# The heads of two feed-forwards without GpSimd, and the squaring of their hidden tiles on ScalarE

## The chip, the cores and the metric

The kernel runs on one core of a Trainium2 chip. The metric is the device time of one launch in microseconds. The kernel before takes 4710.16 us, the median of three runs of 4697.45, 4710.16 and 4712.71 us.

## The reference

Three blocks follow one another over a sequence of 1024 tokens of width 1024: a mixer with three groups of recurrences, a block with a short convolution and an attention, and a block with two gated mixers. The second and the third block each hold a feed-forward with a hidden width of 4096, and the change touches these two alone:

```
m = rmsnorm(h, g_mlp[i])
h = h + jnp.square(jax.nn.relu(m @ w_up[i])) @ w_down[i]
```

```
def rmsnorm(x, g):
    y = xf * lax.rsqrt(jnp.mean(xf * xf, axis=-1, keepdims=True) + EPS)
    return (y * g.astype(jnp.float32)).astype(x.dtype)
```

A token's root factor is the same for all its hidden values, so it can be put on behind the up product: with s = 1/sqrt(mean + eps), relu(u s)^2 is relu(u)^2 s^2, and it is also (relu(u) s)^2.

## The kernel before

Both feed-forwards are built by one function, `feed_forward`, called as "2" and as "3". The residual stream `all_hid` stands in SBUF with channels on the partitions: 8 tiles of 128x1024. All large products are done in three passes, as high*high, low*high and high*low: each operand is rounded to a high part by ScalarE, and VectorE makes the low part as the value less the high part. So nothing can be multiplied before ScalarE and then VectorE have passed over it.

The up product makes the hidden tiles in pairs, 16 pairs of two tiles (128x1024 each). Pairs 0 and 1 are made plainly (`multiply_plain`, line 3068): four blocks u of the weights, 24 matmuls each. From pair 2 on (PLAIN = 2) a pair is a 2x2 block product after Strassen in Winograd's form: seven products j = 0 to 6 (`multiply`, line 3095) of 12 matmuls of 128x512 each, where the right-hand sides are four sums and differences of blocks of x, and the left-hand sides are four sums and differences of blocks of the weights (`combine`). In the kernel before all the weight sums and nine of the ten instructions of the x sums are on GpSimd (POOL); the x sums read copies of the scaled x that ScalarE lays down first (`scale_x`, 12 instructions). The tenth (`t3`, line 3354) is on VectorE. TensorE takes the first products of pair 2 in the order j = 0, 1, 2, 3, ..., and each of j = 1 to 4 waits there for its x sum (`t_low`).

The results of the seven products lie in four PSUM banks (`ff_bank`). ScalarE reads the ones of j = 0, 1, 2 and 6 into `ff_made_out` (`read`, line 3174), VectorE adds those of 3, 4 and 5 (line 3317). TensorE's product 3 uses the bank of product 1 again and so waits for the read of product 1. Then `shape` makes the hidden tile: line 3327 takes max(a, 0) * a, line 3331 multiplies by the row `all_sums`, which holds 1/(mean + eps). SyncE stores the tile to DRAM (`inner`, line 3007).

Order is written out by hand: each engine works off one list of its own, and semaphores tie the lists together. Of the lists these points matter:

- SyncE: for each pair q it stores the first tile, loads the raw up-weights of pair q + 2 (two DMAs of 512 KB into the one buffer `ff_raw`, line 3003), and stores the second tile. The load waits until VectorE has made the low part of the sixth block of pair q + 1 (semaphore `w_low`). After the last pair's predecessor it goes on to `load_y` (line 3027) and `load_w` (line 3017) of the down product: tiles y0, y1, weights w0, y2 to y5, w1, y6 to y9, the store of tile 31, y10 to y13, the store of tile 30, w2.
- ScalarE: a pair's list is read 0, high 0, read 1, high 1, read 2, high 2 to 5, read 6, high 6. A high part of pair q + 1 waits for the same product of pair q, whose weights it replaces.
- The down product (line 3116) makes 32 output parts of 128x1024 in 48 matmuls each, eight parts for each quarter of the hidden tiles. The first part needs y0 to y7 one after another, with 6 matmuls for each.

The row itself is made once: the squares' sums are totalled by TensorE (line 225, 8 matmuls for both feed-forwards), and ScalarE takes Ln (line 233) and Exp (line 235).

Of the kernel before, what the change touches and what calls it, by code (L numbers as in the profile page):

```python
# [2939 lines left out]
def feed_forward(nc, dram, n, hid, gain, up, down, sums):  # L2940
# [8 lines left out]
    with Part(nc, "ff" + n, dram) as p:  # L2949
# [11 lines left out]
        (combined, w_high, w_low, x_high, x_low, scaled, summed_x, third, t_high, t_low, product, act_read, dve_read, shaped, made) = (  # L2961
            p.sem(a) for a in ("combined", "w_high", "w_low", "x_high", "x_low", "scaled", "summed_x", "third", "t_high", "t_low",
# [4 lines left out]
        scale = TokenScale(nc, p, sums, row, power=-1.0, total=acc[:, 0])  # L2967
# [86 lines left out]
        def _(pe):  # L3054
# [17 lines left out]
            def multiply(q, j):  # L3072
# [17 lines left out]
                if q == PLAIN and j in (1, 2, 3, 4):  # L3090
                    pe.wait_ge(t_low, {4: 1, 2: 2, 1: 3, 3: 4}[j])
# [31 lines left out]
        def _(act):  # L3123
            A = nc.scalar.activation
            nc.scalar.preload_act_table_set("natural_log_exp_and_others")

# [23 lines left out]
            def scale_x(h):  # L3150
                A(x_hi[:, 2:4, h, :], cut(hid[:, h, :]), ACT.Copy, scale=gain[:, h:h + 1]).then_inc(scaled, 1)
                lower, g = cut(hid[:, h + H, :]), gain[:, h + H:h + H + 1]
                A(x_hi[:, 4, h, :], lower[:, 1, :], ACT.Copy, scale=g).then_inc(scaled, 1)
                A(x[:, 3, h, :], lower[:, 0, :], ACT.Copy, scale=g).then_inc(scaled, 1)

            def high_t(t, j, what):
                if j == 1:
                    act.wait_ge(summed_x, 1)
                    act.wait_ge(product, products(1) + 3)
                else:  # L3160
                    act.wait_ge(third, 2 * H if j != 3 else 2 * H + 1)
                    act.wait_ge(summed_x, 1)
# [23 lines left out]
            for u in range(2):  # L3186
                high_plain(0, u)
                for h in range(H):
                    high_x(u * H + h)
            high_plain(0, 2)  # L3190
            high_plain(0, 3)
            scale.root(act)
            copy(0, 0)
            for h in range(H):
                scale_x(h)
            high_plain(1, 0)
            high_plain(1, 1)
            copy(0, 1)
            high_plain(1, 2)
            high_plain(1, 3)  # L3200
            copy(1, 0)
            high(PLAIN, 0)
            high_t(0, 4, x[:, 4])
            high_t(1, 2, x[:, 2])
            high(PLAIN, 1)
            high_t(2, 1, t3)
            high_t(3, 3, x[:, 3])
            high(PLAIN, 2)
            copy(1, 1)
# [12 lines left out]
            for i in range(2, 6):  # L3222
# [3 lines left out]
            high_y(6)  # L3226
            high_y(7)
# [21 lines left out]
        def _(pool):  # L3249
            T = nc.gpsimd.tensor_tensor  # L3250

            def combine(q):
                pool.wait_ge(raw_in[0], 16 * q)
                if q > PLAIN:
                    pool.wait_ge(product, products(q - 1) + 2)
                T(wl[:, 1], a11, a21, ALU.subtract).then_inc(combined, 1)
                pool.wait_ge(raw_in[1], 16 * q)
                pool.wait_ge(combined, sums_made(q) + 1)
                T(a21, a21, a22, ALU.add).then_inc(combined, 1)
                if q > PLAIN:  # L3260
                    pool.wait_ge(product, products(q - 1) + 3)
                pool.wait_ge(combined, sums_made(q) + 2)
                T(wl[:, 2], a21, a11, ALU.subtract).then_inc(combined, 1)
                if q > PLAIN:
                    pool.wait_ge(w_low, products(q))
                pool.wait_ge(combined, sums_made(q) + 3)
# [570 lines left out]
```

## Time and profile before

| | |
|---|---|
| median of three runs | 4710.16 us |
| the profiled execution | 4700.76 us, of which its span 4699.0 us |
| TensorE (PE) busy | 4270.1 us, 91% of the span |
| VectorE (DVE) busy | 2091.5 us, 45% |
| ScalarE (ACT) busy | 1603.2 us, 34% |
| GpSimd (POOL) busy | 636.8 us, 14% |
| mean granted TensorE clock | 0.958 of full speed |

The times of one execution are counted from the start of its span. Feed-forward 2 lies from about 2629 to 3315 us, feed-forward 3 from about 3981 us to near the end. Busy shares are means over many stages; for the change it counts where TensorE stands still inside these two stretches. A matmul's own duration in the trace (390 ns) is longer than the distance of two starts, since they overlap; the distance is what counts.

### The profile page before, as it was taken

Reading aid. Unit: us, or ns where it says so; the run is one execution under the profiler, and the core shown is the slowest. Engines: PE = TensorE matmul, PEld = TensorE weight load, DVE = VectorE, ACT = ScalarE, POOL = GpSimd, SP = SyncE. Lnnn points to the kernel's source line nnn. Section 1 sums busy time; section 2 is a strip of 40 time slices with the busy share of each in tenths; the row PEclk is TensorE's granted clock in tenths of the full one; section 3 lists DMA queues with packets and bytes.
Section 4 is the critical chain, followed back from the end, with each engine's and each line's share of the span. In section 5 each row is a group of like instructions: output and inputs, shape, how many; then the busy total and the mean of one; then the engine's idle time right before and its main releaser. Section 6 shows DMA issues by size and latency. Waiting matters only on the chain. (4 is left out here: it accounts for less than half of the span.)

```text
span 4699.0 us, 67316 instructions
## 1 busy us (share of the span) xinstructions
PE 4270.1 (91%) x28429; PEld 3475.5 (74%) x28429; DVE 2091.5 (45%) x2868; ACT 1603.2 (34%) x2680; POOL 636.8 (14%) x508
## 2 busy tenths in 40 slices
PE   7988899987979979899998899999989878999998
PEld 5988889756958858677434688888767676788887
DVE  4544425363345552324443466433442363666333
ACT  3732235242243332311575433222332333433221
POOL 0024400010001100002231332000100001321001
PEclk8989999998989999999999999999999898999999
DMA  3110012122110021111000133421111221234222
GB/s 112 38 60 2 2 41 70 49 65 81 45 36 9 9 78 45 62 42 45 32 10 27 56 115 108 148 95 59 53 33 41 57 47 45 94 112 153 82 94 72
DMA packets 323010, 284.91 MB, mean 61 GB/s; under 512 B 19569, under 2 KB 288145, under 8 KB 322594
## 3 DMA queue, kind: packets, MB, share of 16 engines
q1 hardware_dynamic: 322722, 280.76, 19.3%
q8 instruction: 218, 3.57, 0.3%
q14 instruction: 70, 0.57, 0.0%
HBM read 204.55 MB, written 55.31 MB: 55 GB/s over the span
## 5 line engine op out<-in xcount | busy, mean ns | idle before, releaser
L3116 PE MATMUL ff_acc<-ff_x_hi_rounded,ff_wh_rounded 128*128 128x512 f32 x1024 | 399.8, 390 | 5.2 <-DVE ff_x_rounded L3335 5.2
L3116 PE MATMUL ff_acc<-ff_x_rounded,ff_wh_rounded 128*128 128x512 f32 x1024 | 399.2, 390 | 0.0
L3116 PE MATMUL ff_acc<-ff_x_hi_rounded,ff_wl_rounded 128*128 128x512 f32 x1024 | 399.2, 390 | 0.0
L3095 PE MATMUL ff_bank<-ff_x_hi_rounded,ff_wh_rounded 128*128 128x512 f32 x784 | 308.8, 394 | 17.0 <-issue 9.6
L3095 PE MATMUL ff_bank<-ff_x_hi_rounded,ff_wl_rounded 128*128 128x512 f32 x784 | 308.0, 393 | 0.0
L3095 PE MATMUL ff_bank<-ff_x_rounded,ff_wh_rounded 128*128 128x512 f32 x784 | 308.0, 393 | 0.0
L3116 PEld LDWEIGHTS ff_acc<-ff_x_hi_rounded,ff_wh_rounded 128*128 128x128 f32 x1024 | 192.7, 188 | 46.8 <-DVE ff_x_rounded L3335 6.9
L3184 ACT ACTIVATE ff_wh_rounded<-ff_wl 128x512 fp32r<-128x512 f32 x128 | 80.6, 632 | 417.2 <-DMA ff_wl<-w_mlp_dram 207.7
L3116 PEld LDWEIGHTS ff_acc<-ff_x_hi_rounded,ff_wl_rounded 128*128 128x128 f32 x1024 | 192.7, 188 | 39.9
L3116 PEld LDWEIGHTS ff_acc<-ff_x_rounded,ff_wh_rounded 128*128 128x128 f32 x1024 | 192.6, 188 | 39.9
L3405 DVE TENSOR_TENSOR all_hid<-all_hid,ff_acc 128x1024 f32<-128x1024 f32 x64 | 78.2, 1221 | 303.0 <-PE ff_acc L3116 303.0
L1936 PE MATMUL mid_acc<-b1h_hn_hi_rounded,mid_w_hi_rounded 128*128 128x352 f32 (+1 forms) x528 | 186.8, 354 | 4.7 <-DVE mid_w_rounded L1918 4.7
L3095 PEld LDWEIGHTS ff_bank<-ff_x_hi_rounded,ff_wh_rounded 128*128 128x128 f32 x784 | 149.0, 190 | 49.3 <-issue 18.6
L1936 PE MATMUL mid_acc<-b1h_hn_hi_rounded,mid_w_rounded 128*128 128x352 f32 (+1 forms) x528 | 183.8, 348 | 0.0
L1936 PE MATMUL mid_acc<-b1h_hn_rounded,mid_w_hi_rounded 128*128 128x352 f32 (+1 forms) x528 | 183.4, 347 | 0.0
L3095 PEld LDWEIGHTS ff_bank<-ff_x_rounded,ff_wh_rounded 128*128 128x128 f32 x784 | 148.9, 190 | 31.5
L3095 PEld LDWEIGHTS ff_bank<-ff_x_hi_rounded,ff_wl_rounded 128*128 128x128 f32 x784 | 149.1, 190 | 31.1
L3342 DVE TENSOR_TENSOR ff_wl_rounded<-ff_wl,ff_wh_rounded 128x512 fp32r<-128x512 f32 x128 | 98.5, 778 | 141.5 <-ACT ff_wh_rounded L3184 138.8
L1936 PE MATMUL pa_acc<-b1h_hn_hi_rounded,pa_w_hi_rounded 128*128 128x352 f32 x432 | 147.3, 341 | 12.0 <-DVE b1h_hn_rounded L1922 12.0
L477 PE MATMUL pb_acc<-b1h_hn_hi_rounded,pb_w_hi_rounded 128*128 128x352 f32 x408 | 132.8, 325 | 16.1 <-ACT b1h_hn_hi_rounded L381 16.1
L1936 PE MATMUL pa_acc<-b1h_hn_hi_rounded,pa_w_rounded 128*128 128x352 f32 x432 | 140.0, 324 | 0.0
L1936 PE MATMUL pa_acc<-b1h_hn_rounded,pa_w_hi_rounded 128*128 128x352 f32 x432 | 139.8, 324 | 0.0
(642 smaller groups left out, 10628.6 us busy)
## 6 DMA issues: line engine op xcount, KB each, us to landing
inner<-ff_made_out SPq DMA_DIRECT2D x64, 512.0 KB, 2.6
ff_x<-inner SPq DMA_DIRECT2D x64, 512.0 KB, 5.6
ff_wl<-w_down_dram SPq DMA_DIRECT2D x64, 256.0 KB, 3.1
ff_wl<-w_mlp_dram SPq DMA_DIRECT2D x64, 256.0 KB, 3.0
ff_raw<-w_up_dram SPq DMA_DIRECT2D x30, 512.0 KB, 4.2
ff_raw<-w_mlp_dram SPq DMA_DIRECT2D x30, 512.0 KB, 4.3
mid_w<-w_in_dram SPq DMA_DIRECT2D x104, 128.0 KB, 2.7
pa_w<-w_in_dram SPq DMA_DIRECT2D x72, 128.0 KB, 2.7
```

The costliest lines, as they stand in the source:

```text
L477: mm = nc.tensor.matmul(acc[s][:, c, :width], rounded(l[:, k, :]), rounded(r[:, k, at]), start=(k == 0 and j == 0), stop=(k == k_tiles - 1 ...
L1936: mm = self.nc.tensor.matmul(self.acc[s][:, c, :width], rounded(l[:, k, :]), rounded(r[:, k, at]), start=(k == 0 and j == 0), stop=(k == K ...
L3095: mm = M(to, rounded(a[:, j, h, :]), rounded(b[:, j, h, :]), start=(j in (0, 1, 5) and h == 0 and i == 0), stop=(h == H - 1 and i == 2), s ...
L3116: mm = M(acc[:, s, c, :], rounded(a[:, s, k, :]), rounded(b[:, at, c * W2:(c + 1) * W2]), start=(k == 0 and i == 0), stop=(k == KD - 1 and ...
L3184: A(rounded(w_hi[:, s, a * H:(a + 1) * H, :]), w[:, s, a * H:(a + 1) * H, :], ACT.Copy).then_inc(d_high, 1)
L3342: T(rounded(w[:, s, part, :]), w[:, s, part, :], rounded(w_hi[:, s, part, :]), ALU.subtract).then_inc(d_low, 1)
L3405: T(cut(hid[:, f, :]), cut(hid[:, f, :]), acc[:, s, :, :], ALU.add).then_inc(acc_free, 1)
```

## The change

In both feed-forwards:

- GpSimd does nothing any more before the down product's sums of squares. The four weight sums of a pair go to VectorE, in two pieces behind the low parts 0 and 1 of the pair. The x sums go to VectorE as 16 instructions of 128x512 (`sum_x`), which scale and subtract in one; ScalarE's `scale_x` shrinks from 12 instructions to 4 and stands ahead of the row's Ln and Exp. The t_low order becomes 4, 2, 3, 1.
- ScalarE and VectorE take x tiles 0 and 1 and x tile 0 ahead of the first weight block.
- The loading of a table of ScalarE's functions at the head (line 3125) goes.
- Hidden tiles: the row holds 1/sqrt(mean + eps) (the default power). In pairs 0 and 1 ScalarE rectifies as it copies out of PSUM and VectorE multiplies by the row (`weigh_plain`); in the others one instruction of VectorE takes max(a, 0) * row. In all pairs ScalarE squares the tile in place (`square_made`), and the store waits for that. In the pairs' lists the square of a pair's first finished tile stands behind high 5 of the next pair's weights, that of its second tile behind high 1 of the round after; the last ones stand behind the reads of pair 15 and behind the high parts of y0 to y7, w0 and w1.
- At the start of the down product the high and low parts of y6 and y7 stand ahead of w1 and of the last tiles' shaping.

```
-        scale = TokenScale(nc, p, sums, row, power=-1.0, total=acc[:, 0])
+        scale = TokenScale(nc, p, sums, row, total=acc[:, 0])
...
-            nc.scalar.preload_act_table_set("natural_log_exp_and_others")
...
             def copy(q, i):
                 act.wait_ge(product, products(q) + 2 * (i + 1))
-                A(cut(made_out[:, q % 2, i, :]), plain_acc[q, i], ACT.Copy).then_inc(act_read, 1)
+                A(cut(made_out[:, q % 2, i, :]), plain_acc[q, i], ACT.Relu).then_inc(act_read, 1)
+
+            def square_made(q, i):
+                act.wait_ge(shaped, 2 * q + (1 if i == first_half(q) else 2))
+                A(made_out[:, q % 2, i, :], made_out[:, q % 2, i, :], ACT.Square).then_inc(made, 1)
...
                     high(q + 1, j)
+                    if j == 1:
+                        square_made(q - 1, 1 - first_half(q - 1))
+                    if j == 5:
+                        square_made(q, 1)
             for j in range(3):
                 read(LAST, j)
+            square_made(LAST - 1, 0)
             high_y(0)
...
+            def combine(q, j):
+                if j == 1:
+                    for a in range(2):
+                        dve.wait_ge(raw_in[a], 16 * q)
+                    if q > PLAIN:
+                        dve.wait_ge(product, products(q - 1) + 2)
+                    T(wl[:, 1], a11, a21, ALU.subtract).then_inc(combined, 1)
+                    dve.wait_ge(combined, sums_made(q) + 1)
+                    T(a21, a21, a22, ALU.add).then_inc(combined, 1)
+                else:
+                    if q > PLAIN:
+                        dve.wait_ge(product, products(q - 1) + 3)
+                        dve.wait_ge(w_low, products(q))
+                    dve.wait_ge(combined, sums_made(q) + 2)
+                    T(wl[:, 2], a21, a11, ALU.subtract).then_inc(combined, 1)
+                    dve.wait_ge(combined, sums_made(q) + 3)
+                    T(fourth[:, :, :], a12, wl[:, 2], ALU.subtract).then_inc(combined, 1)
...
+            def sum_x(to, k, c, less):
+                V.scalar_tensor_tensor(to, hid[:, k, c * W2:(c + 1) * W2], gain[:, k:k + 1], less, ALU.mult, ALU.subtract).then_inc(summed_x, 1)
...
-                a = made_out[:, q % 2, i, :]
-                V.scalar_tensor_tensor(a, a, 0.0, a, ALU.max, ALU.mult).then_inc(shaped, 1)
-                dve.wait_ge(shaped, 2 * q + (1 if i == first_half(q) else 2))
-                if q == 0:
-                    dve.wait_ge(scale.rooted, 1)
-                T(a, a, row, ALU.mult).then_inc(made, 1)
+                a = made_out[:, q % 2, i, :]
+                V.scalar_tensor_tensor(a, a, 0.0, row, ALU.max, ALU.mult).then_inc(shaped, 1)
```

SyncE's and TensorE's lists keep their instructions and their order. Two places of the other lists bear on the time.

VectorE at the head of feed-forward 2, before. `ff_wl_rounded` are low parts of the weights, `ff_x_rounded` of x or an x sum, `ff_square<-ff_x_hi` is the sum t3, and the pairs of rows on `ff_made_out` are the shaping in two steps:

```order
L3293 TENSOR_TENSOR ff_wl_rounded<-ff_raw,ff_wh_rounded 128x512
L3304 SCALAR_TENSOR_TENSOR ff_x_rounded<-all_hid,all_par,ff_x_hi_rounded 128x2x512 x4
L3293 TENSOR_TENSOR ff_wl_rounded<-ff_raw,ff_wh_rounded 128x512
L3304 SCALAR_TENSOR_TENSOR ff_x_rounded<-all_hid,all_par,ff_x_hi_rounded 128x2x512 x4
L3293 TENSOR_TENSOR ff_wl_rounded<-ff_raw,ff_wh_rounded 128x512 x2
L3327 SCALAR_TENSOR_TENSOR ff_made_out<-ff_made_out 128x1024
L3331 TENSOR_TENSOR ff_made_out<-ff_made_out,all_sums 128x1024
L3293 TENSOR_TENSOR ff_wl_rounded<-ff_raw,ff_wh_rounded 128x512 x2
L3354 TENSOR_TENSOR ff_square<-ff_x_hi 128x2048
L3327 SCALAR_TENSOR_TENSOR ff_made_out<-ff_made_out 128x1024
L3331 TENSOR_TENSOR ff_made_out<-ff_made_out,all_sums 128x1024
L3293 TENSOR_TENSOR ff_wl_rounded<-ff_raw,ff_wh_rounded 128x512 x2
```

And in the changed kernel, where the rows on `all_par` of 128x512 are `sum_x`:

```order
L3303 SCALAR_TENSOR_TENSOR ff_x_rounded<-all_hid,all_par,ff_x_hi_rounded 128x2x512
L3274 TENSOR_TENSOR ff_wl_rounded<-ff_raw,ff_wh_rounded 128x512
L3303 SCALAR_TENSOR_TENSOR ff_x_rounded<-all_hid,all_par,ff_x_hi_rounded 128x2x512 x3
L3274 TENSOR_TENSOR ff_wl_rounded<-ff_raw,ff_wh_rounded 128x512
L3303 SCALAR_TENSOR_TENSOR ff_x_rounded<-all_hid,all_par,ff_x_hi_rounded 128x2x512 x4
L3274 TENSOR_TENSOR ff_wl_rounded<-ff_raw,ff_wh_rounded 128x512 x2
L3307 SCALAR_TENSOR_TENSOR ff_x<-all_hid,all_par,ff_x_hi 128x512 x4
L3307 SCALAR_TENSOR_TENSOR ff_square<-all_hid,all_par,ff_x_hi 128x512 x4
L3323 TENSOR_TENSOR ff_made_out<-ff_made_out,all_sums 128x1024
L3307 SCALAR_TENSOR_TENSOR ff_x<-all_hid,all_par,ff_x 128x512 x4
L3274 TENSOR_TENSOR ff_wl_rounded<-ff_raw,ff_wh_rounded 128x512 x2
L3307 SCALAR_TENSOR_TENSOR ff_x<-all_hid,all_par,ff_x 128x512 x4
```

One x tile has gone ahead of the first weight block, sixteen `sum_x` stand around the first tile's weighing, and t3 as one large instruction is gone.

ScalarE around the last pair of feed-forward 2, before: reads of `ff_bank`, the high parts of the hidden tiles (`ff_x_hi_rounded<-ff_x 128x1024`) and of the down weights (`ff_wh_rounded<-ff_wl`, twice):

```order
L3174 ACTIVATE ff_made_out<-ff_bank 128x512 x3
L3178 ACTIVATE ff_x_hi_rounded<-ff_x 128x1024 x2
L3184 ACTIVATE ff_wh_rounded<-ff_wl 128x512 x2
L3178 ACTIVATE ff_x_hi_rounded<-ff_x 128x1024 x4
L3184 ACTIVATE ff_wh_rounded<-ff_wl 128x512 x2
L3174 ACTIVATE ff_made_out<-ff_bank 128x512
L3178 ACTIVATE ff_x_hi_rounded<-ff_x 128x1024 x3
```

And in the changed kernel, where `ff_made_out<-ff_made_out` is a square:

```order
L3170 ACTIVATE ff_made_out<-ff_bank 128x512 x3
L3163 ACTIVATE ff_made_out<-ff_made_out 128x1024
L3174 ACTIVATE ff_x_hi_rounded<-ff_x 128x1024 x2
L3180 ACTIVATE ff_wh_rounded<-ff_wl 128x512 x2
L3174 ACTIVATE ff_x_hi_rounded<-ff_x 128x1024 x6
L3180 ACTIVATE ff_wh_rounded<-ff_wl 128x512 x2
L3170 ACTIVATE ff_made_out<-ff_bank 128x512
L3163 ACTIVATE ff_made_out<-ff_made_out 128x1024 x2
```

A square now stands between the three reads and the first y tile, SyncE's store and all its later loads wait for it, and y6 and y7 are ahead of w1.

## Rows read from the trace of the kernel before

**Rows 1.** Waits of TensorE, head of feed-forward 2; us in total, times, longest.

```profile
...
PE ff_bank L3095 <- DVE ff_x_rounded L3311: 3.5, 1, 3.5
PE ff_acc L3068 <- DVE ff_x_rounded L3304: 2.2, 1, 2.2
PE ff_acc L3068 <- DVE ff_wl_rounded L3293: 1.2, 1, 1.2
PE ff_bank L3068 <- DVE ff_wl_rounded L3293: 1.1, 1, 1.1
```

**Rows 2.** Waits of TensorE, 2700 to 2965 us.

```profile
PE ff_bank L3095 <- issue: 4.6, 1, 4.6
```

**Rows 3.** Waits of TensorE, head of feed-forward 3.

```profile
...
PE ff_bank L3095 <- issue: 5.0, 1, 5.0
PE ff_bank L3095 <- DVE ff_x_rounded L3311: 3.9, 1, 3.9
...
```

**Rows 4.** Timeline of TensorE, feed-forward 2: start us, duration us, instruction [idle <-releaser].

```profile
...
2659.54 0.39 PE L3068 MATMUL ff_bank<-ff_x_rounded,ff_wh_rounded 128*128 128x512 f32 x1
...
2715.11 0.39 PE L3095 MATMUL ff_bank<-ff_x_hi_rounded,ff_wh_rounded 128*128 128x512 f32 x1
...
```

**Rows 5.** Timeline of TensorE, feed-forward 3, the same two places.

```profile
...
4011.14 0.39 PE L3068 MATMUL ff_bank<-ff_x_rounded,ff_wh_rounded 128*128 128x512 f32 x1
...
4068.84 0.39 PE L3095 MATMUL ff_bank<-ff_x_hi_rounded,ff_wh_rounded 128*128 128x512 f32 x1
...
```

**Rows 6.** Windows: length, PE, PEld, DVE, ACT, POOL busy; PEclk, DMA share, GB/s.

```profile
2690.00:2695.00 5.00, 4.23 (x13) 3.38 (x14) 4.97 (x5) 0.05 (x1) 0.00 (x0) 0.71 0.00 0
2955.00:2960.00 5.00, 5.00 (x24) 4.15 (x23) 2.97 (x4) 4.11 (x5) 0.00 (x0) 1.00 1.04 413
4325.00:4330.00 5.00, 2.40 (x6) 1.94 (x7) 4.79 (x5) 0.00 (x0) 0.00 (x0) 0.71 0.90 365
```

**Rows 7.** Timeline of ScalarE, head of feed-forward 2.

```profile
...
2629.13 1.28 ACT L3125 ACT_TABLE_LOAD   x1 [3.39 <-PEq L155]
2632.04 0.63 ACT L3133 ACTIVATE ff_wh_rounded<-ff_raw 128x512 fp32r<-128x512 f32 x1 [1.62 <-DMA ff_raw<-w_up_dram]
...
2701.47 0.63 ACT L3144 ACTIVATE ff_wh_rounded<-ff_raw 128x512 fp32r<-128x512 f32 x1 [11.43 <-DMA ff_raw<-w_up_dram]
2702.01 0.58 ACT L3174 ACTIVATE ff_made_out<-ff_bank 128x512 f32<-128x512 f32 x1
...
```

**Rows 8.** Timeline of VectorE, head of feed-forward 2.

```profile
...
2659.73 2.92 DVE L3293 TENSOR_TENSOR ff_wl_rounded<-ff_raw,ff_wh_rounded 128x512 fp32r<-128x512 f32 x2 [7.09 <-ACT ff_wh_rounded L3133]
...
2665.87 5.62 DVE L3327 SCALAR_TENSOR_TENSOR ff_made_out<-ff_made_out 128x1024 f32<-128x1024 f32 x1
...
2695.74 1.89 DVE L3299 TENSOR_TENSOR ff_wl_rounded<-ff_raw,ff_wh_rounded 128x512 fp32r<-128x512 f32 x3
...
```

**Rows 9.** Timeline of SyncE: the loads of the up-weights of pairs 3, 6, 7.

```profile
...
2697.65 0.93 SPq L3003 DMA_DIRECT2D ff_raw<-w_up_dram  x2
...
2752.98 0.94 SPq L3003 DMA_DIRECT2D ff_raw<-w_up_dram  x2
...
2772.02 0.93 SPq L3003 DMA_DIRECT2D ff_raw<-w_up_dram  x2
...
```

**Rows 10.** Groups of VectorE, 2710 to 2945 us: busy us, mean ns | idle.

```profile
...
L3299 DVE TENSOR_TENSOR ff_wl_rounded<-ff_raw,ff_wh_rounded 128x512 fp32r<-128x512 f32 x51 | 34.9, 684 | 0.0
L3327 DVE SCALAR_TENSOR_TENSOR ff_made_out<-ff_made_out 128x1024 f32<-128x1024 f32 x25 | 30.6, 1222 | 0.4
...
```

**Rows 11.** Page, costliest groups: the down product's first line.

```profile
...
L3116 PE MATMUL ff_acc<-ff_x_hi_rounded,ff_wh_rounded 128*128 128x512 f32 x1024 | 399.8, 390 | 5.2 <-DVE ff_x_rounded L3335 5.2
...
```

**Rows 12.** Timeline of SyncE, start of the down product.

```profile
...
2948.47 1.14 SPq L3027 DMA_DIRECT2D ff_x<-inner  x2
...
```

**Rows 13.** Timeline of ScalarE, start of the down product.

```profile
2953.57 1.06 ACT L3178 ACTIVATE ff_x_hi_rounded<-ff_x 128x1024 fp32r<-128x1024 f32 x1 [1.02 <-DMA ff_x<-inner]
```

**Rows 14.** Timeline of VectorE, start of the down product.

```profile
...
2972.60 3.49 DVE L3335 TENSOR_TENSOR ff_x_rounded<-ff_x,ff_x_hi_rounded 128x1024 fp32r<-128x1024 f32 x3
...
```

More of the change, by code:

```diff
@@ L2960, in feed_forward @@
         stored = [p.sem(f"stored{s}") for s in range(2)]
-        (combined, w_high, w_low, x_high, x_low, scaled, summed_x, third, t_high, t_low, product, act_read, dve_read, shaped, made) = (
-            p.sem(a) for a in ("combined", "w_high", "w_low", "x_high", "x_low", "scaled", "summed_x", "third", "t_high", "t_low",
+        (combined, w_high, w_low, x_high, x_low, scaled, summed_x, t_high, t_low, product, act_read, dve_read, shaped, made) = (
+            p.sem(a) for a in ("combined", "w_high", "w_low", "x_high", "x_low", "scaled", "summed_x", "t_high", "t_low",
                                "product", "act_read", "dve_read", "shaped", "made"))
@@ L3184, in high_w @@
                     A(rounded(w_hi[:, s, a * H:(a + 1) * H, :]), w[:, s, a * H:(a + 1) * H, :], ACT.Copy).then_inc(d_high, 1)
[L3186 to L3189, printed above, removed]
+            high_x(0)
+            high_x(1)
+            high_plain(0, 0)
+            for k in range(2, H):
+                high_x(k)
+            high_plain(0, 1)
+            for k in range(H, KD):
+                high_x(k)
             high_plain(0, 2)
             high_plain(0, 3)
+            for h in range(H):
+                scale_x(h)
             scale.root(act)
             copy(0, 0)
-            for h in range(H):
-                scale_x(h)
             high_plain(1, 0)
             high_plain(1, 1)
+            square_made(0, 0)
             copy(0, 1)
@@ L3200, in _ @@
             high_plain(1, 3)
-            copy(1, 0)
-            high(PLAIN, 0)
             high_t(0, 4, x[:, 4])
             high_t(1, 2, x[:, 2])
+            high_t(2, 3, x[:, 3])
+            square_made(0, 1)
+            high(PLAIN, 0)
+            copy(1, 0)
             high(PLAIN, 1)
-            high_t(2, 1, t3)
-            high_t(3, 3, x[:, 3])
             high(PLAIN, 2)
+            high_t(3, 1, t3)
+            square_made(1, 0)
             copy(1, 1)
@@ L3221, in _ @@
             high_w(0)
-            for i in range(2, 6):
+            for i in range(2, KD):
                 high_y(i)
@@ L3250, in _ @@
             T = nc.gpsimd.tensor_tensor
[L3252 to L3266, printed above, removed]
-                T(fourth[:, :, :], a12, wl[:, 2], ALU.subtract).then_inc(combined, 1)
-            for h in range(H):
-                pool.wait_ge(scaled, 3 * h + 2)
-                T(x[:, 4, h, :], x_hi[:, 3, h, :], x_hi[:, 2, h, :], ALU.subtract).then_inc(third, 1)
-                pool.wait_ge(third, 2 * h + 1)
-                T(x[:, 2, h, :], x_hi[:, 4, h, :], x[:, 4, h, :], ALU.subtract).then_inc(third, 1)
-            pool.wait_ge(scaled, 3 * H)
-            pool.wait_ge(third, 2 * H)
-            T(x[:, 3], x[:, 3], x[:, 2], ALU.subtract).then_inc(third, 1)
-            for q in range(PLAIN, PAIRS):
-                combine(q)
             for f in range(KD):
@@ L3371, in _ @@
                     low(q + 1, j)
+                    if j < 2:
+                        combine(q + 1, j + 1)
                 read(q, 3)
@@ L3388, in _ @@
             shape(LAST, 1)
-            for i in range(3, 6):
+            for i in range(3, KD):
                 low_y(i)
```

72 lines of the change are left out of this document (38 added, 34 removed).

## Prediction

> **What bounds the kernel now.** I read the page's table of busy shares first: TensorE is busy 91% of the span, the others half of it or less. So the next view is who TensorE waits for inside the two feed-forwards. In feed-forward 2 the reader is to see few rows: at the head 2.2 us until the first low x tile, 1.2 and 1.1 us for low parts of pair 1's weights, 3.5 us for the low part of an x sum [rows 1], then 4.6 us of "issue" [rows 2], and after that nothing until the down product. Pairs 3 to 14 stand exactly 19.04 us apart (2772.02 less 2752.98) [rows 9]; that is 84 matmuls at 0.2267 us, TensorE at its own pace. Feed-forward 3 shows the same waits, 3.9 and 5.0 us for the two large ones [rows 3]. Each has one more at the start of the down product, 5.2 us for both together [rows 11].
>
> The timeline of TensorE gives the whole loss of the head in one subtraction. From the last matmul of pair 0 (2659.54) to the first of pair 3 (2715.11) there are 181 steps (the 96 matmuls of pair 1 and the 84 of pair 2 lie between); at 0.2267 us they take 41.0 us, and the rows are 55.6 us apart. So 14.5 us are lost: 10.4 in the four waits named, the rest in slow stretches behind the waits [rows 1, 2, 4]. The granted clock says the same, 0.71 of full over the window from 2690, where the engine had just stood still 3.5 us; a mean of its two levels, 2.4 and 1.2 GHz [rows 6]. In feed-forward 3 the same two places are 57.7 us apart, a loss of 16.7 us [rows 5].
>
> "Issue" names nobody, so the other engines' timelines have to. ScalarE takes a high part of pair 3's weights at 2701.47 after 11.4 us of idling for the DMA of `ff_raw`, and reads PSUM at 2702.01 [rows 7]; that read is the one that frees the bank of product 1, which product 3 writes. TensorE goes on at its end, 2702.6. The DMA was issued at 2697.65 [rows 9], because VectorE made low parts 3, 4 and 5 of pair 2 only from 2695.74 on [rows 8]. So both large waits have one cause: VectorE comes late. It comes late because it shares with GpSimd: one instruction of 128x1024 at 2665.87 took 5.62 us [rows 8], the same form takes 1.22 us in the steady pairs [rows 10].
>
> **The change part by part.** *The first product.* ScalarE idles 1.62 us for the first weights, behind a table load of 1.28 us [rows 7]. Now it makes the high parts of x0 and x1 there (1.06 us each, the row of the same form [rows 13]), and VectorE the low part of x0. The first product then hangs on the weights: 2632.04 + 0.63 + 0.69 = 2633.4 instead of 2635.2. These 1.7 us are at half clock. If the clock rises at the same instant as before, they are worth half, if it follows the start, all. I take 1.0 us (bounds 0.8 and 1.8).
>
> The table load itself costs nothing where it stands, since the DMA ended later. The trace has 1.28 us of load and then the DMA's wait. The Trainium skill ("ScalarE: Activation LUTs", What ACT_TABLE_LOAD costs) counts a drain of 1.38 us with each load, 2.66 us in all. By that rule on the path, the head would gain up to 2.7 us a time instead of 1.0, 3.4 us more for both; here the DMA row overrules it.
>
> *VectorE at the head.* It gets 16 `sum_x`. No row shows this form at 128x512; the nearest are 0.68 us for two tensors of 128x512 [rows 10] and 1.22 us as upper end (twice the elements). That is 10.9 us at the nearest, 19.5 us at most; I take the nearest. They fall where VectorE idled 7.1 us until 2659.73 and 4.9 us before its first shaping, and it loses t3, the waits beside GpSimd (5.62 - 1.22 = 4.4 us on one instruction alone) and three instructions of shaping. Counting its list through from 2633, at 1.22 us for 1024 elements and 0.64 for 512: the low x tiles end at 2642.5, the first eight `sum_x` at 2648.8, the weighing and four more at 2653, low parts 0 and 1 of pair 1 at 2654.1. Pair 1 is wanted at 2658.7 (2659.8 less the 1.0). There are 4.6 us to spare, so the 1.1 us wait goes; even at 1.22 us each it is late by about 1.3 us. Low parts 2 and 3 follow the third product's end at 2661.8, wanted at 2669.6. The three x sums' low parts (2.2 us each alone) end by 2671, the weight sums (four of 0.69) by 2674, low 1 and 2 at 2675.3, the fourth x sum at 2679.5; wanted for product 1 at 2683.2. So the 1.2 and the 3.5 us go, with the slow stretch behind.
>
> *What is late next.* Low 3 to 5 of pair 2 stand behind the weighing of pair 1's last tile, which needs pair 1's last product. From that product's end: ScalarE's copy 1.1, weighing 1.2, three low parts 1.9 [rows 8], the DMA 3.8 (2701.47 less 2697.65), the high part 0.6, the read 0.6, in all 9.3 us. TensorE has three products meanwhile, 3 x 2.72 = 8.2 us. A wait of 1.3 us stays in front of product 3 instead of 4.6. Then one more: ScalarE's next high part needs a weight sum, which VectorE makes only when both halves are in; with the second half a good 1 us behind the first, I get 0.7 us before product 4. In feed-forward 3 the load took some 0.4 us more, so 2.6 us there. Waits of 1.1 to 1.2 us left no slow stretch before, so I count none. Bounds for these waits: 0, and 5 us a head if transfers land 2 us later and the clock falls.
>
> Head: 14.5 + 1.0 - 2.0 = 13.5 us, and 16.7 + 1.0 - 2.6 = 15.1 us.
>
> *Steady pairs.* VectorE: two steps of shaping a tile become one (-2.4 us a pair), four weight sums come (+2.7). ScalarE: two squares, +2.1 us of 19. Neither is near 19 us, so only chains count, and I cost this at nothing. The cover: ScalarE's read of product 2 now stands behind a weight sum of VectorE, a high part and a square, 0.7 + 0.6 + 1.1 = 2.4 us after product 1; product 2 lasts 2.72 and product 3 another 2.72, before which nobody wants that read. What is queued behind the new waits on VectorE (for both halves of `ff_raw`) are low 1 and the reads of products 3 to 5, wanted a product or more later. The load of the next weights is issued behind a store that now waits for a square: product 5's end + 0.6 + 1.1 + 0.4 = 2.1 us. The bound above nothing is the first rival.
>
> The same page of the Trainium skill (Rules for kernel authors) says to put maximum and multiplication on VectorE rather than ScalarE, as VectorE is up to 3 times as fast in bf16. In fp32 the rows don't bear it out: 1.06 us on ScalarE [rows 13] against 1.22 on VectorE [rows 10] for 1024 elements. By the rule the two squares of a pair would slow ScalarE, but with 8 of 19 us busy the sum is the same.
>
> *Start of the down product.* Pair 15 starts at 2715.11 + 12 x 19.04 = 2943.6; its products end at 2946.4, ..., 2951.9 (third), 2962.8. SyncE loaded y0 at 2948.47 [rows 12]; now tile 28's store ahead of it waits for a square behind the third read: 2951.9 + 0.6 + 1.1 + 0.4 = 2954.0, so 5.5 us later. y0 landed 5.1 us after its issue (2953.57) [rows 13], now 2959.1. The queue then moves 413 GB/s at a DMA share of 1.04 [rows 6], 1.27 us for 512 KB. The weights w0 are third: 2961.6, high and low part to 2963.2; the product starts 0.4 us late. y7 is tenth: 2959.1 + 9 x 1.27 = 2970.5, ready at 2973.0; TensorE, with 1.36 us a tile, wants it at 2972.7. With small waits on the way the first part ends at about 2974.9. Before it ended at 2976.6: VectorE shaped the last tile ahead of y6, whose low part began at 2972.60 and ended at 2973.8 [rows 14], and two tiles of 1.36 us follow. That is 1.7 us gained. In feed-forward 3 the wait also cost a slow stretch (clock 0.71 from 4325 [rows 6]): six or seven matmuls at twice the distance, 1.3 us. Against it: w2 is queued behind the last two stores and y10 to y13, 3.4 MB from 2974.7 on, and lands about 2985, a moment after it could be used without loss (wanted, split, at 2985.8). I take 0.7 us for it, bounds 0 and 3. Net 1.0 and 2.3 us.
>
> **Sum.** 13.5 + 15.1 + 1.0 + 2.3 = 31.9 us. Against the profiled execution (4700.76) that is 4668.9 us; this execution was 9.4 us under the median of the runs, so against the median of 4710.16 it is 4678 us.
>
> **The rivals.** *A, slower: the store in front of the raw load.* Each pair the load shares the DMA engines with a store issued 0.4 us ahead (1.8 us before), and ScalarE's and VectorE's lists are blocked while they wait for it. From product 5's end, ScalarE must have done the next high 0 and read 1 when product 2 of the next pair ends, 4 x 2.72 = 10.9 us. Less 2.1 until the issue and 1.2 for the two instructions, the load may take 7.6 us; the row shows 3.8. Each us beyond 7.6 costs 1 us in 26 pairs. It decides from about 8.8 us, where the gain is eaten; at 9.5 us the kernel takes 4678 + 50 = 4728 us. Against it: two loads and a store are 1.5 MB, 3.8 us at 413 GB/s. *B, the down product starves.* The loads are 5.5 us later and TensorE waits for all of it, as the queue is already full before: 5.5 + 1.7 us each, with slow stretches 8.5; 32 - 17 gives 15 less, 4693 us. For it: the DMA share of 1.04. Against it: the wait before was for VectorE, not for a landing. *C, the heads stay bound by VectorE.* `sum_x` at 1.22 us and slow landings: 1.3 + 5 us a head come back, and the clock falls behind one of the waits (1.5): 32 - 16 = 16, 4694 us; with B in part it reaches no change. *D, the change doesn't do what it says:* without GpSimd at work the VectorE instructions stay long. Then it wasn't sharing, and the head would gain only the waits at pair 1, 4700 us. The same form at 1.22 us in steady pairs speaks against it.
>
> **How the numbers follow.** Forecast 0.70, A 0.05, B 0.12, C 0.09, D 0.04. The range must reach B and C, 4694, with some us for how the runs scatter (the three differ by 15 us), and down to 4661: start worth 1.8, no waits left, w2 in time, and the runs at the low end. So 4661 to 4700 us. A gain of 0.3% (14 us, what this kernel's measurement can tell) ends at 4696: the forecast, most of B and half of C are faster, 0.84; within 0.3% 0.10; slower 0.06.
>
> **What would show it.** TensorE's waits of 3.5 and 4.6 us gone, one of 1 to 2 us before product 3 of pair 2, and pair 3 starting 72 to 73 us after the head's first matmul at 2629.17, where it was 86. No VectorE instruction of 128x1024 over 1.3 us at the head. Pairs 3 to 14 still 19.04 us apart; anything more is A. At the down product y0 landing 5 to 6 us later relative to pair 15, and still a wait under 1.5 us in all; more is B. I'd be wrong in the sum if the heads gained less than 10 us each or if a pair grew by 0.5 us.

## The result and the profile after

The changed kernel took 4673.7 us in the median of five runs (4662.06 to 4680.76), the kernel before 4710.16 in the median of five on the same chip (4696.03 to 4712.74). The ratio is 0.9929, with an interval of 0.9908 to 0.9950: 0.5% to 0.9% less time. The forecast was 4678. The profiled execution took 4662.06 us with a span of 4660.3, against 4700.76 before.

The two profiles are 38.7 us apart, and the change didn't bring all of it. The feed-forwards' first matmul stands at 2625.69 us now, at 2629.17 before: 3.5 us were won before anything that the change touches, and in the profiles of all the kernels below this point lies anywhere between 2625.7 and 2644.5. So I measure inside, from the first matmul of the row total (L225) to the fourth output part of the down product. Every column is us of TensorE's starts: from L225 to the first matmul of pair 0, of pair 1, of pair 3; from there to pair 15; from pair 15 to the second, third and fourth part of the down product; and the sum of head, pairs and down product's start.

| kernel, feed-forward | pair 0 | pair 1 | pair 3 | pairs 3-14 | 2nd | 3rd | 4th | sum |
|---|---|---|---|---|---|---|---|---|
| before, 2 | 6.01 | 31.83 | 85.94 | 228.48 | 33.13 | 44.01 | 54.89 | 369.31 |
| before, 3 | 6.01 | 31.84 | 88.07 | 228.48 | 34.49 | 45.38 | 56.26 | 372.81 |
| after, 2 | 4.16 | 26.58 | 68.86 | 228.48 | 31.98 | 44.67 | 55.64 | 352.98 |
| after, 3 | 4.24 | 27.97 | 70.51 | 228.48 | 30.84 | 44.16 | 55.14 | 354.13 |

The change is worth 16.3 + 18.7 = 35.0 us; 31.9 were forecast. In the profile of the changed kernel TensorE's waits in the head of feed-forward 2 are these (what waited, for whom: us in total, times, longest), where [rows 1] and [rows 2] had 3.5, 2.2, 1.2, 1.1 and 4.6:

```profile
PE ff_acc L225 <- PEq L155: 5.8, 1, 5.8
PE ff_bank L3095 <- issue: 0.9, 1, 0.9
PE ff_acc L3068 <- DVE ff_wl_rounded L3274: 0.4, 1, 0.4
```

The 5.8 us are the wait for the total itself, which the kernel before has too; 0.4 us are inside pair 0. Behind it only the 0.9 us before product 3 of pair 2 are left (1.05 if counted from the distance of the two starts; 1.3 in feed-forward 3). The same view of the start of the down product, first in feed-forward 2, then in 3:

```profile
PE ff_acc L3116 <- DVE ff_wl_rounded L3341: 2.1, 2, 1.6
PE ff_acc L3116 <- DVE ff_x_rounded L3334: 0.7, 2, 0.5
```
```profile
PE ff_acc L3116 <- DVE ff_wl_rounded L3341: 2.3, 1, 2.3
PE ff_acc L3116 <- DVE ff_x_rounded L3334: 0.2, 1, 0.2
```

On the page, [rows 11] had 5.2 us here, for the low part of a hidden tile. The total is no smaller now (5.3 us), but most of it is one wait for the low part of w2 in each feed-forward:

```profile
L3116 PE MATMUL ff_acc<-ff_x_hi_rounded,ff_wh_rounded 128*128 128x512 f32 x1024 | 399.1, 390 | 5.3 <-DVE ff_wl_rounded L3341 4.3
```

VectorE's timeline at the head (start, us for all that the row names, count) shows the new x sums at 0.68 us each (2.73 for four), and nothing over 1.3 us at 128x1024, where [rows 8] had one of 5.62:

```profile
2639.89 2.73 DVE L3307 SCALAR_TENSOR_TENSOR ff_x<-all_hid,all_par,ff_x_hi 128x512 f32<-128x512 f32 x4
2642.54 2.73 DVE L3307 SCALAR_TENSOR_TENSOR ff_square<-all_hid,all_par,ff_x_hi 128x512 f32<-128x512 f32 x4
2645.19 1.22 DVE L3323 TENSOR_TENSOR ff_made_out<-ff_made_out,all_sums 128x1024 f32<-128x1024 f32 x1
...
2676.43 1.89 DVE L3298 TENSOR_TENSOR ff_wl_rounded<-ff_raw,ff_wh_rounded 128x512 fp32r<-128x512 f32 x3
```

The last row is low parts 3 to 5 of pair 2, which stood at 2695.74 in [rows 8]: 66.6 us after the first matmul then, 50.7 now. ScalarE's timeline answers to [rows 7]: it waits 4.20 us for the raw weights instead of 11.43.

```profile
2682.02 0.63 ACT L3142 ACTIVATE ff_wh_rounded<-ff_raw 128x512 fp32r<-128x512 f32 x1 [4.20 <-DMA ff_raw<-w_up_dram]
```

The first step of the chain that made VectorE late before is not in the rows read so far. Behind the instruction of 5.62 us it made the last low parts of pair 1 only at 2672.66; the raw weights of pair 2 were issued at 2673.98, behind them, and ScalarE had them at 2677.70. Then the low parts of two x sums took 6.56 us beside GpSimd's weight sums. In the changed kernel the same two take 4.49 us with GpSimd idle. Before, then after:

```profile
2672.66 1.29 DVE L3293 TENSOR_TENSOR ff_wl_rounded<-ff_raw,ff_wh_rounded 128x512 fp32r<-128x512 f32 x2
...
2680.17 6.56 DVE L3311 TENSOR_TENSOR ff_x_rounded<-ff_x,ff_x_hi_rounded 128x2048 fp32r<-128x2048 f32 x2 [0.64 <-ACT ff_x_hi_rounded L3163]
```
```profile
2656.37 4.49 DVE L3311 TENSOR_TENSOR ff_x_rounded<-ff_x,ff_x_hi_rounded 128x2048 fp32r<-128x2048 f32 x2 [1.04 <-ACT ff_x_hi_rounded L3155]
```

The wait at the start of pair 1 had another cause: there VectorE had idled 7.1 us for ScalarE [rows 8], which was busy with the twelve copies of `scale_x` until 2659.07. No run separates what these copies cost from the rest.

### The profile page after: what moved, and what is told of

Same layout as the page of the kernel before. It is cut to its first block and busy times, and to the rows that moved or that the text cites. A ratio compares the mean times of both kernels' runs of the same rounds, so it can differ in the third digit from the quotient of the medians.

```text
span 4660.3 us, 67248 instructions
## 1 busy us (share of the span) xinstructions
PE 4258.0 (91%) x28429; PEld 3467.6 (74%) x28429; DVE 2079.5 (45%) x2946; ACT 1653.5 (35%) x2726; POOL 442.1 (9%) x378
```

## The experiments

Each is a kernel of its own; "after" is the changed kernel. The table gives, for both feed-forwards, the start of pair 3 and of the fourth output part (counted as above), and the sum; pairs 3 to 14 took 228.48 us in all of them but one. The last column is the median where a kernel was run several times (before, after, after again, both) and the time of a single run elsewhere.

| kernel | pair 3 | 4th part | both sums | us |
|---|---|---|---|---|
| before | 85.9, 88.1 | 54.9, 56.3 | 742.1 | 4710.16 |
| after | 68.9, 70.5 | 55.6, 55.1 | 707.1 | 4673.7 |
| after, again | 70.6, 68.7 | 56.0, 57.4 | 709.6 | 4672.49 |
| shaping alone | 82.3, 84.5 | 54.4, 54.4 | 732.6 | 4692.6 |
| sums alone | 71.9, 72.2 | 52.0, 52.0 | 705.0 | 4671.11 |
| weight sums on GpSimd | 68.5, 69.1 | 57.3, 55.4 | 707.1 | 4677.14 |
| weights first | 72.9, 70.1 | 55.9, 54.7 | 710.6 | 4671.44 |
| table load put back | 70.6, 70.9 | 56.0, 55.4 | 709.8 | 4670.38 |
| GpSimd adding 128x512 | 82.7, 84.1 | 55.6, 54.7 | 734.0 | 4695.86 |
| GpSimd adding 128x1024 | 88.7, 87.8 | 57.5, 56.8 | 747.8 | 4724.44 |
| loads before stores | 70.6, 69.1 | 53.5, 52.8 | 703.0 | 4667.93 |
| y0 ahead of tile 28 | 68.9, 69.3 | 51.7, 51.7 | 698.5 | 4674.86 |
| late square | 68.9, 68.5 | 57.7, 55.5 | 731.4 | 4698.24 |
| both | 68.9, 67.2 | 51.7, 51.7 | 696.5 | 4660.25 |

"After" and "after, again" are the same program: a head moves by 1.8 us from one execution to the next, and both sums by 2.5. Less than that tells nothing here. The times scatter by more (the point where the feed-forwards begin), so the sums decide; the kernel before, run beside them, took 4702.85 to 4710.16 us.

**Which half pays.** Two kernels do one part of the change each. *Shaping alone* is the kernel before with the scaling on VectorE and the square on ScalarE. *Sums alone* is the changed kernel with the shaping of before; it keeps all the rest of the change too: the x tiles ahead of the first weights, no table load, and y6 and y7 ahead of w1.

```diff
-A(cut(made_out[...]), plain_acc[q, i], ACT.Copy)      # shaping alone
+A(cut(made_out[...]), plain_acc[q, i], ACT.Relu)
-V.scalar_tensor_tensor(a, a, 0.0, a, ALU.max, ALU.mult); T(a, a, row, ALU.mult)
+V.scalar_tensor_tensor(a, a, 0.0, row, ALU.max, ALU.mult)    # and square_made on ScalarE
```

> The kernel before with the shaping alone changed: row of the single root, one VectorE instruction a tile, ScalarE squares in place; all sums stay where they were, on GpSimd. Stages are read from TensorE's starts in feed-forward 2: head (first matmul of the row's total to first matmul of pair 3) 85.9 us before, 68.9 changed; pairs 3 to 14 228.5 in both; start of the down product (pair 15 to the fourth part) 54.9 before, 55.6 changed. Theory (VectorE was late because it shares with GpSimd): the head stays at 82 to 86 us, and an instruction of VectorE of several us still stands beside GpSimd's large one; the start of the down product gets the wait for its third weights, 1 to 3 us. Time against before: within 6 us. Rival (the shorter shaping carries the gain): head under 75 us, about 4675 us in all.

> The changed kernel with the old shaping in two VectorE steps and no squares on ScalarE; the sums stay on VectorE. Theory: the head is 70 to 72 us (two tiles' second steps of 1.2 us stand before the load of pair 3), pairs 3 to 14 stay 228.5, and the start of the down product is shorter than in both kernels, 52 to 53.5 us, since no load waits for a square: in all as fast as the changed kernel or up to 4 us faster. Rival (the shaping is needed for VectorE to carry the sums): head over 78 us, or pairs over 19.1 us each.

Measured against before: 9.5 us for the shaping, 37.2 for the sums, 35.0 for both. The parts don't add up. Alone, the shaping wins 3.6 us in each head; on top of the sums it wins 3.0 and 1.7, or 1.3 and 3.4 against the second profile of after. And the squares cost time at the down product: its fourth part starts 3.7 and 3.2 us later with them than without.

Two expectations of *shaping alone* missed. Its time was 13 us under that of the kernel before beside it (4705.77), where at most 6 were expected. And the wait for w2 did not come, though the squares are in: its fourth part starts at 54.4 us in both feed-forwards, earlier than in the changed kernel. In it y6 and y7 do not stand ahead of w1, so the squares of the last tiles are done earlier: ScalarE takes w2 40.3 us after pair 15's start, in the changed kernel 43.2 us (feed-forward 2). *Sums alone* has that reordering without the squares and no wait for w2 either. So the late w2 comes of the two together.

The shaping pays some of that back in the head, where the sums alone leave this one wait of 2.8 us (waits of that kernel; the starts are 2.93 us apart):

```profile
PE ff_bank L3095 <- issue: 2.8, 1, 2.8
```

With both it is 0.9. So everything but the shaping brings the whole gain; what the shaping adds (2.2 us more time against one profile of after, 4.6 against the other) is at best nothing.

**Which sums.** *Weight sums on GpSimd* is the changed kernel with `combine` given back to GpSimd from pair 2 on.

```diff
+pool: for q in range(PLAIN, PAIRS): combine(q)     # as before
-dve:  combine(q, 1); combine(q, 2)                 # four 128x512 a pair
```

> The changed kernel with the weight sums back on GpSimd in all pairs; the x sums stay on VectorE. Theory: GpSimd then runs beside VectorE only in pair 2, while low parts of the x sums are made: head 69 to 73 us against 68.9, pairs 3 to 14 228.5, so the x sums are the part that pays. Rival (the weight sums pay): head over 78 us.

Nothing came back: 707.1 against 707.1. The weight sums are free on either engine, though they do lengthen VectorE's instructions: the weighing of pair 0's second tile takes 2.31 us beside them instead of 1.22, at a place where it is not wanted at once. The 35 us are those of `t3`, the x sums and the scaled tiles, and of the earlier first product (below).

**Sharing (rival D).** Two kernels have the changed order and a GpSimd that adds a tile to itself, which nobody reads, beside VectorE's x sums. The only difference between them is the size of one addition, with the number of additions halved to match.

```diff
+pool.wait_ge(scaled, 2)
+nc.gpsimd.memset(idle, 0.0)
+for n in range(24): T(idle, idle, idle, ALU.add)   # idle is 128x512
+for n in range(12): ...                            # in the other kernel 128x1024
```

> The changed kernel, and GpSimd works for nothing at the head: 24 additions of 128x512 in a tile of its own, from the second scaled x tile on (about 31 us). It measures the sharing alone. Theory: VectorE's two-input instructions of 128x512 beside it take 1.1 us or more instead of 0.69, the head grows by 5 to 15 us from 68.9. Rival (VectorE was late for its place in the order, not for sharing): durations 0.69 and 1.22 as without, head 69 us.

> The changed kernel, and GpSimd works for nothing at the head in large pieces: 12 additions of 128x1024, about 29 us, against 24 of 128x512 in the earlier run, where VectorE's instructions beside them grew. Theory (VectorE and GpSimd take turns by whole instructions): a VectorE instruction with two inputs waits for the end of the one on GpSimd, so single instructions last up to 2.4 us and more than with small pieces, and the head is 82 us or more. Rival (they share the width evenly, whatever the pieces): VectorE's mean durations as with the small pieces, head 82.7 and 84.1 us within 1 us.

GpSimd's timeline of the first, then VectorE's:

```profile
2643.51 38.26 POOL L3266 TENSOR_TENSOR ff_idle<-ff_idle 128x512 f32<-128x512 f32 x24
```
```profile
2643.78 5.87 DVE L3314 SCALAR_TENSOR_TENSOR ff_x<-all_hid,all_par,ff_x_hi 128x512 f32<-128x512 f32 x4
...
2655.36 2.06 DVE L3330 TENSOR_TENSOR ff_made_out<-ff_made_out,all_sums 128x1024 f32<-128x1024 f32 x1
```

And of the second, where GpSimd stops at 2685.75:

```profile
2657.59 28.16 POOL L3266 TENSOR_TENSOR ff_idle<-ff_idle 128x1024 f32<-128x1024 f32 x12
```
```profile
2665.00 9.27 DVE L3314 SCALAR_TENSOR_TENSOR ff_square<-all_hid,all_par,ff_x_hi 128x512 f32<-128x512 f32 x4
2674.20 2.91 DVE L3330 TENSOR_TENSOR ff_made_out<-ff_made_out,all_sums 128x1024 f32<-128x1024 f32 x1
...
2687.43 2.73 DVE L3314 SCALAR_TENSOR_TENSOR ff_x<-all_hid,all_par,ff_x 128x512 f32<-128x512 f32 x4
```

Four x sums take 2.73 us alone, 5.87 beside additions of 38.26 / 24 = 1.59 us, and 9.27 beside additions of 28.16 / 12 = 2.35 us. One x sum then takes 0.8 us more than its 0.68 beside the small additions and 1.6 us more beside the large ones, though it moves the same elements each time. The weighing, twice as long by itself (1.22 us), gets the same addition: 2.06 beside the small ones and 2.91 beside the large ones. D is refuted: the length of VectorE's instructions comes from GpSimd's work. By it alone pair 3 starts 14 us later, and with the larger additions 17 to 20 us, so the whole gain of a head is gone. The 5.62 us of [rows 8], 4.4 more than alone, stood beside GpSimd's one large instruction of the kernel before:

```profile
2663.94 6.46 POOL L3276 TENSOR_TENSOR ff_x<-ff_x 128x2048 f32<-128x2048 f32 x1
```

**The first product.** *Weights first* is the changed kernel with the old order of ScalarE's and VectorE's first instructions, *table load put back* has the preload of before.

```diff
-high_x(0); high_x(1); high_plain(0, 0)             # weights first
+high_plain(0, 0); high_x(0); high_x(1)             # and low_plain ahead of low_x
+nc.scalar.preload_act_table_set("natural_log_exp_and_others")   # the other kernel
```

> The changed kernel with the old order at the very start: the first weight block ahead of x tiles 0 and 1 on ScalarE and of x tile 0 on VectorE. It asks why the start was worth 4.0 and 2.6 us where 1.0 was forecast. Counted from the first matmul of the row's total, pair 0 begins at 4.2 us and pair 1 at 26.6 and 28.0 in the changed kernel, at 6.0 and 31.8 before (with a wait of 1.2 in it). Theory (the earlier start keeps the clock from staying low): pair 0 begins at 5.8 to 6.0, the clock rises 11 to 12 us after the total's start as before, pair 1 begins at 29.5 to 30.6 and pair 3 at 71.5 to 73. Rival (only the shift itself counts): pair 1 at 28.3 to 29, pair 3 at 70.6 to 71.

> The changed kernel with the table load back at the head. Theory: the load takes 1.28 us before the high part of x0, which pushes the second x tile 0.7 us over the landing of the first weights; pair 0 begins at 4.9 us instead of 4.2, pair 3 0.5 to 1.5 us later. By the Trainium skill (ScalarE: Activation LUTs, What ACT_TABLE_LOAD costs) it would be 2.66 us with the drain: pair 0 at 6.2 us. Rival (it is hidden by the load of the weights as before): no difference.

With the weights first, pair 0 starts at 5.95 and 5.80 us instead of 4.16 and 4.24, as expected. What that costs at pair 3 is unclear: 4.1 us in feed-forward 2, nothing in feed-forward 3. TensorE is at half clock at first, and windows of the profiles (busy times, then granted clock, DMA share, GB/s) show how early it is granted the full one, after and before:

```profile
2625.70:2629.80 4.10, 3.74 (x4) 1.14 (x4) 1.98 (x3) 3.52 (x4) 0.00 (x0) 0.50 0.67 190
2632.00:2634.00 2.00, 2.00 (x11) 1.63 (x10) 2.00 (x4) 2.00 (x3) 0.00 (x0) 1.00 0.03 8
```
```profile
2635.20:2640.00 4.80, 4.80 (x11) 3.75 (x12) 4.80 (x5) 4.80 (x6) 0.00 (x0) 0.50 0.02 3
```

Pair 1 shows the instant: it starts at 26.2 to 28.3 us in the executions with the early first product, at 27.7 and 30.5 in those with the late one, at 31.8 before (of which 1.2 were a wait). So the early start brings between nothing and 4 us, as the clock is granted sooner or later. Whether the early start itself brings the early clock is open: one late start had the full clock from pair 0's first product on, the other stayed at half pace until 11.6 us after the first matmul of the total, nearly as before.

With the table load pair 0 starts at 4.74 us, 0.6 later than after, and both sums are 2.7 more than the first profile of after and 0.3 more than the second: not to be told from nothing. The Trainium skill ("ScalarE: Activation LUTs", What ACT_TABLE_LOAD costs) counts 2.66 us for a switch to a different set, 1.28 for the load and 1.38 for a drain. The trace agrees with the load, 1.28 us, but shows no drain: the next activation begins 0.02 us behind its end. This load repeats the set that is already in place. About half of the 1.28 us lies in the wait for the first weights.

```profile
2630.36 1.28 ACT L3125 ACT_TABLE_LOAD   x1 [3.39 <-PEq L155]
2631.66 2.19 ACT L3148 ACTIVATE ff_x_hi_rounded<-all_hid,all_par 128x1024 fp32r<-128x1024 f32 x2
```

**The store in front of the raw load (rival A).** *Late square* moves one square of a pair one product later, so that the store and the load behind it are issued about 3 us later in each pair.

```diff
-if j == 5: square_made(q, 1)
+if j == 6: square_made(q, 1)
```

> The changed kernel with the square of a pair's first finished tile behind high 6 instead of high 5. It tries the threshold of the rival that didn't come (the store in front of the raw load): the store and the load behind it then follow product 6. The load was issued 2.1 us after product 5 and took 4.6 us; now it is issued 5.4 us after. Theory: ScalarE's next high 0 and read 1 end later than product 3 wants them; a pair grows from 19.04 to 19.4 to 19.8 us, pairs 3 to 14 to 233 to 238 us from 228.5. Rival (the wait is hidden, the lists have more slack than was counted): 228.5.

The pairs took 241.02 and 239.81 us instead of 228.48, about 1 us each of the twelve. TensorE's waits, in a stretch of 150 us:

```profile
PE ff_bank L3095 <- ACT ff_made_out L3170: 3.4, 7, 0.9
```

That is before product 3; TensorE's starts show a smaller delay of 0.2 us before product 4 as well, which the count had not. SyncE issues the load at 2807.53, and ScalarE goes on with it 4.6 us later:

```profile
2807.53 1.26 SPq L3003 DMA_DIRECT2D ff_raw<-w_up_dram  x2
```
```profile
2812.13 0.63 ACT L3142 ACTIVATE ff_wh_rounded<-ff_raw 128x512 fp32r<-128x512 f32 x1 [3.81 <-DMA ff_raw<-w_up_dram]
```

A's mechanism is real. Its threshold lies a few tenths of a us lower than the rows put it, since the pair came out at 20.0 to 20.1 us where 19.4 to 19.8 were expected. The changed kernel stays clear of it: its load is issued 2.1 us after product 5's end, and 7.6 are free against the 4.4 to 5.4 that it takes.

**The start of the down product.** *Loads before stores* issues y10 to y13 of the down product ahead of the last two stores; w2 stays behind these. *y0 ahead of tile 28* adds that y0, y1 and w0 are issued ahead of the store of tile 28, which waits for a square.

```diff
-for i in range(6, 10): load_y(i)                   # loads before stores
-store(LAST, 1)
-for i in range(10, RING): load_y(i)
+for i in range(6, RING): load_y(i)
+store(LAST, 1)
 store(LAST, 0)
-store(LAST - 1, second); load_y(0); load_y(1); load_w(0)   # y0 ahead, added
+load_y(0); load_y(1); load_w(0); store(LAST - 1, second)
```

> The changed kernel, on SyncE y10 to y13 ahead of the stores of the last two tiles, which wait for squares. Theory: w2 is late because y10 to y13 and two stores are in front of it; with y10 to y13 issued some 10 us earlier, while the queue is half idle, w2 lands in time: the waits of 1.8 and 2.4 us before the third output part go, start of the down product 53.6 and 52.8 us instead of 55.6 and 55.1. Rival (w2 is late since it waits for the end of the first part): unchanged.

> As the last, and also y0, y1 and w0 ahead of the store of tile 28, which waits for a square. Theory: the small waits at the first part go too (0.6, 0.4 and 0.6 us): start of the down product 52.0 to 52.5 us, what the kernel without squares on ScalarE takes (51.98), 8 us in all under the changed kernel. Rival (the store then holds up what follows it, y2 to y5): waits of 1 us or more at the third to sixth tile.

Both came out as expected in the stretch that they touch, the second 0.3 us better. With y10 to y13 out of the queue before the stores, w2 has only these in front of it, and TensorE's wait for w2 (1.8 and 2.4 us) is gone: the fourth part starts at 53.5 and 52.8; with y0 ahead as well, at 51.68, with no wait at all. The one time of the second, 4674.86, doesn't show it: in its profile the first matmul stands at 2644.47 us, 19 us later than after and ahead of every instruction that this edit moves. Why this stretch scatters so I did not find out. The last kernel has the same edit and shows the gain in its median.

**Again, and both ends mended.** The changed kernel once more, and a version with y0 ahead in which ScalarE's and VectorE's lists have parts 3 to 5 of pair 2 ahead of pair 1's last copy and weighing:

```diff
-copy(1, 1); high(PLAIN, 3..6)
+high(PLAIN, 3..5); copy(1, 1); high(PLAIN, 6)
-weigh_plain(1, 1); low(PLAIN, 3..6)
+low(PLAIN, 3..5); weigh_plain(1, 1); low(PLAIN, 6)
```

> The changed kernel once more, as it was timed first, beside the next one on the same chip. Ratio to the kernel before 0.990 to 0.995; stages as in its first profile, but for the moment at which the clock rises in pair 0, which moved pair 1's start between 26.4 and 28.3 us in the runs with this head.

> The changed kernel with both moves on SyncE (y0, y1, w0 ahead of the store of tile 28, y10 to y13 ahead of the last two stores), and in pair 2 the high and low parts 3 to 5 ahead of the copy and the weighing of pair 1's last tile. Theory: the load of pair 3's weights goes 1.8 us earlier, the wait of 1.1 to 1.3 us before product 3 goes, start of the down product 51.7 us: both feed-forwards take 9 to 11 us less than in the changed kernel, ratio to before 0.989 to 0.992 where the changed kernel has 0.993. Rival (the next wait takes its place): the head as in the changed kernel.

The changed kernel again: 4672.49 us in the median of six (4665.98 to 4684.94), ratio 0.9932 (0.9913 to 0.9952). Both ends mended: 4660.25 us (4654.07 to 4664.18), ratio 0.9901 (0.9884 to 0.9918), against 4707.34 for the kernel before. Its sums are 10.7 and 13.1 us under the two profiles of after. This version beats both kernels. TensorE's waits from feed-forward 2's head to its down product:

```profile
PE ff_acc L225 <- PEq L155: 5.8, 1, 5.8
PE ff_acc L3068 <- DVE ff_wl_rounded L3275: 0.5, 1, 0.5
```

## Why the prediction was right

*The bound, and the cause of the two large waits.* Right. VectorE came late because it shared with GpSimd, and in the two kernels where GpSimd adds beside it, it is late again by that alone. That the waits of 3.5 and 4.6 us themselves come of it is read from the chain in the trace.

*The head's loss and the waits that stay.* 14.5 - 2.0 and 16.7 - 2.6 were forecast, 12.5 and 14.1 us. Less the part that pair 1's start explains, 13.1 and 14.9 were measured; the waits, with small delays, cost 1.5 and 1.7 us. The wait of 1.3 us before product 3 of pair 2 was 1.05 and 1.3. Of the 0.7 us forecast before product 4, 0.2 and 0.3 came.

*The first product.* The mechanism held: x0 and x1 now lie in the wait for the weights, and pair 0 starts 1.85 and 1.77 us earlier (1.7 forecast). The size did not. I took 1.0 us of it, with bounds of 0.8 and 1.8; measured at pair 1, less the 1.2 us of the wait that went, are 4.0 and 2.6. This is the term that was mis-sized most: it came out 4.7 us above the forecast for both, the head's waits and losses 1.4 above, the down product 2.9 below, and that makes the 3.1 us by which the sum fell short. That the sum came so near is in part luck, since two of its misses cancel. The clock was granted earlier by more than the start moved: TensorE's steps are at half pace until 11.7 us before, until 5.2 and 8.2 after. Whether the earlier start was the reason stays open. The forecast of 72 to 73 us for pair 3 was 68.9 and, in feed-forward 3, 70.5.

*Steady pairs.* Exact: 228.48 us in both kernels. Rival A was priced near the truth and did not arise. The 3.8 us by which the forecast judged it are from a load with no store near it; with the store 0.4 us ahead it is 4.4 to 5.4 us.

*The down product.* y0 was to be issued 5.5 us later against pair 15: it was issued at 2933.38, 10.35 us after pair 15's start, where [rows 12] give 4.88. The second part was to start 1.7 and 3.0 us earlier, and did by 1.15 and 3.65. The part that was wrong is w2: 0.7 us were counted, 1.8 and 2.4 measured. SyncE's timeline shows why:

```profile
2954.52 0.32 SPq L3007 DMA_DIRECT2D inner<-ff_made_out  x1
2954.94 2.15 SPq L3027 DMA_DIRECT2D ff_x<-inner  x4
2957.14 0.51 SPq L3007 DMA_DIRECT2D inner<-ff_made_out  x1
2957.70 32.41 SPq L3017 DMA_DIRECT2D ff_wl<-w_down_dram  x7
```
```profile
2966.20 1.38 ACT L3180 ACTIVATE ff_wh_rounded<-ff_wl 128x512 fp32r<-128x512 f32 x2 [8.54 <-DMA ff_wl<-w_down_dram]
```

The stores that wait for the last squares hold back y10 to y13 and w2 alike, so that these go out together, and ScalarE can use w2 only 8.5 us after its issue. Net the term was a loss of 0.75 in feed-forward 2 (a gain of 1.0 was forecast) and a gain of 1.1 in 3 (2.3 forecast). That is rival B in small: landings, not VectorE, bound this stretch now. The bounds of the w2 term (0 and 3) held it.

*Rivals.* B in part, C not at all (the x sums took 0.68 us, the near end), D refuted.

## What to carry to other kernels

Here GpSimd was no spare room for elementwise work while VectorE was on the path: if VectorE has idle time of its own nearby, try the work there, and compare single VectorE instructions beside GpSimd's with the same form alone to see what the sharing costs. When a chain is changed, follow it to the stores: a store that waits for one more step holds every load behind it in the same queue, and issuing loads ahead of it brought 4.0 and 3.5 us here (fourth part at 51.68 instead of 55.64 and 55.14). Time the parts of a change one by one, since here one of them, the shaping, was worth nothing beside the rest.

## What was not expected of the hardware

An fp32 VectorE instruction with two tensor inputs that runs beside GpSimd additions is longer by an amount that goes by the size of GpSimd's instruction and not by its own. Beside additions of 128x512 (1.59 us each) it was 0.8 us: 0.68 became 1.47 and 1.22 became 2.06. Beside additions of 128x1024 (2.35 us) it was 1.6 to 1.7: 0.68 became 2.32 and 1.22 became 2.91. That the two engines take turns by whole instructions is my reading of these numbers; no trace shows the turns themselves.

TensorE's clock went from 1.2 to 2.4 GHz at another moment in each execution of the same program: pair 1 started at 26.58 us in one profile of after and at 28.21 in the other, with pair 0 at 4.16 and 4.29.

A 512 KB load issued 0.4 us behind a 512 KB store took 4.4 to 5.4 us until ScalarE used it (steady pairs of the changed kernel; 4.6 in the rows of late square). Issued 1.8 us behind the store, as in the kernel before, it took 3.6 to 4.2 us, no more than the 3.8 of [rows 7, 9], where no store was issued for 21 us ahead of it.
